# Turning the cross memory's rows: from TensorE to VectorE's 32x32 blocks

## What is computed

```
h = h + merged @ w_out[l]
u = rms_norm(h, norm_xattn_g[l])
mem_n = rms_norm(mem, norm_mem_g[l])               # mem: 256 rows of width 1024
h = h + memory_cross_attention(u, mem_n, ...)

# memory_cross_attention
q = (u @ w_xq) * 128 ** -0.5                       # 4 heads of width 128
kv = mem_n @ w_xkv                                 # keys and values of the 256 rows
s = q k^T per head;  p = softmax(s);  o = p v
return o @ w_xo
```

## Time and profile before

| | |
|---|---|
| median of 3 runs | 1354.56 us (1354.35 to 1354.66) |
| the profiled execution | 1354.18 us |
| its span, first to last instruction | 1352.4 us |
| TensorE busy | 1336.3 us, 99% |
| TensorE weight loads | 1092.6 us, 81% (they overlap the matmuls) |
| VectorE busy | 934.5 us, 69% |
| ScalarE busy | 585.6 us, 43% |
| GpSimd busy | 71.4 us, 5% |
| granted TensorE clock, mean | 1.00 |
| phase w_out | about 295 to 352 us from the span's start |

### The profile page before, as it was taken

The page is one execution under the profiler, slowest core; times in us unless marked ns, Lnnn a source line. Parts: engine busy times, 40 slices in busy tenths (PEclk is TensorE's granted clock), DMA queues, the critical chain, the costliest instruction groups (busy, mean ns, idle before and its releaser), DMA issues.

```text
span 1352.4 us, 17616 instructions
## 1 busy us (share of the span) xinstructions
PE 1336.3 (99%) x6397; PEld 1092.6 (81%) x6397; DVE 934.5 (69%) x1494; ACT 585.6 (43%) x987; POOL 71.4 (5%) x60
## 2 busy tenths in 40 slices
PE   7999999999999999999999999999999999999998
PEld 6787777778888888888888888888888888888886
DVE  7768888785576543355445562598889988995685
ACT  7435655564455432114433344734343433333234
POOL 1000000102002000000013300000000000000000
PEclk9999999999999999999999999999999999999999
DMA  5333233243323333323333333322233223223332
GB/s 163 94 93 79 74 77 84 63 125 109 109 79 94 94 104 113 93 63 111 106 94 93 94 110 93 97 79 84 81 97 94 83 70 95 85 76 109 96 107 94
DMA packets 224104, 127.02 MB, mean 94 GB/s; under 512 B 21234, under 2 KB 214851, under 8 KB 224034
## 3 DMA queue, kind: packets, MB, share of 16 engines
q1 hardware_dynamic: 222418, 123.47, 31.8%
q10 hardware_dynamic: 1616, 2.62, 0.6%
HBM read 123.98 MB, written 2.10 MB: 93 GB/s over the span
## 4 chain that ended last, share of the span: by engine, by line
PE 94%; DVE 3%; ACT 2%; issue 1%; ACTq 0%; DVEq 0%
PE lin L663 26%; PE lin L666 25%; PE lin L667 25%; PE ob L1081 1%; PE sc L746 1%; PE sc L1037 1%; PE sc L1040 1%; PE sc L1041 1%; PE tr L759 1%; PE ob L783 1%; PE sc L770 1%; PE tr L1040 1%; PE lin L1040 1%; PE lin L1041 1%; PE tr L1041 1%
## 5 line engine op out<-in xcount | busy, mean ns | idle before, releaser
L1700 DVE TENSOR_TENSOR wl<-raw,wh 128x1024 fp32r<-128x1024 f32 (+2 forms) x235 | 287.6, 1231 | 64.4 <-ACT wh L1214 59.7
L1214 ACT ACTIVATE wh<-raw 128x1024 fp32r<-128x1024 f32 (+2 forms) x235 | 239.0, 1022 | 132.7 <-DMA raw<-in_w_mlp_dram 44.7
L663 PE MATMUL lin<-uh,wh 128*128 128x512 f32 x624 | 251.2, 402 | 1.3 <-DVE ul L1753 0.9
L667 PE MATMUL lin<-uh,wl 128*128 128x512 f32 x624 | 243.3, 390 | 0.0
L666 PE MATMUL lin<-ul,wh 128*128 128x512 f32 x624 | 243.1, 390 | 0.0
L663 PE MATMUL lin<-vh,wh 128*128 128x512 f32 x512 | 202.6, 396 | 0.2 <-DVE te L2320 0.2
L666 PE MATMUL lin<-vl,wh 128*128 128x512 f32 x512 | 199.6, 390 | 0.0
L667 PE MATMUL lin<-vh,wl 128*128 128x512 f32 x512 | 199.3, 389 | 0.0
L663 PEld LDWEIGHTS lin<-uh,wh 128*128 128x128 f32 x624 | 117.2, 188 | 29.7 <-issue 4.5
L666 PEld LDWEIGHTS lin<-ul,wh 128*128 128x128 f32 x624 | 117.3, 188 | 25.7 <-issue 2.9
L667 PEld LDWEIGHTS lin<-uh,wl 128*128 128x128 f32 x624 | 117.1, 188 | 24.7
(11 more groups left out here) (546 smaller groups left out, 2078.3 us busy)
## 6 DMA issues: line engine op xcount, KB each, us to landing
raw<-in_w_in_dram SPq DMA_DIRECT2D x100, 512.0 KB, 3.8
raw<-in_w_mlp_dram SPq DMA_DIRECT2D x64, 512.0 KB, 3.9
raw<-in_w_out_dram SPq DMA_DIRECT2D x16, 512.0 KB, 3.6
raw<-in_w_xkv_dram SPq DMA_DIRECT2D x8, 512.0 KB, 3.7
raw<-in_w_proj_b_dram SPq DMA_DIRECT2D x8, 512.0 KB, 3.7
raw<-in_w_proj_a_dram SPq DMA_DIRECT2D x8, 512.0 KB, 3.7
xtok<-in_x_dram ACTq DMA_DIRECT2D x4, 512.0 KB, 4.9
raw<-in_w_mla_out_dram SPq DMA_DIRECT2D x4, 512.0 KB, 3.5
```

What stands on the lines that cost most here:

```text
L663: ins = pe.matmul(o, wh[:, slot, at], xh_, start=start, stop=False)
L667: return pe.matmul(o, wl[:, slot, at], xh_, start=False, stop=stop)
L1214: act.activation(wh[:, c.slot(4), 0:size], raw[:, c.slot(2), 0:size], ACT.Copy).then_inc(hi_made, 1)
L1700: dve.tensor_tensor(wl[:, c.slot(4), 0:size], raw[:, c.slot(2), 0:size], wh[:, c.slot(4), 0:size].bitcast(F32), ALU.subtract).then_inc(lo_ ...
```

## The change

`MEM_TURNS`, `turn_memory` and TensorE's calls of it are gone; w_out's jobs run without turns between their matmuls. VectorE turns the memory instead, straight from `memtok` into `memt`, a view of `xp` as 8 feature tiles of 128 x 256. One instruction turns 32 partitions by 512 elements: 16 blocks of 32x32, one for each feature tile and row group. There are 16 of them, five in step m = 0 of w_out, four each in m = 1 and 2, three in m = 3 (`MEM_BLOCKS`), behind the low part of the step's chunk and of the h tile and ahead of the sum to h. VectorE waits for `mem_scaled` at each step. The last one raises `mt_ready`, which now counts to 1.

ScalarE makes all eight `memh` tiles in step m = 3, behind `mt_ready` and ahead of the split of step m = 4. VectorE makes all eight `meml` tiles in step m = 4, behind the chunk's and the h tile's low part and ahead of the sum of job 4. Both read `memt` in on-chip memory where they read a PSUM bank.

```diff
--- before.py
+++ after.py
@@ -109,7 +109,7 @@
 W_ORDER = (("w", 0), ("w", 1), ("w", 2), ("w", 3), ("w", 4), ("k", 0), ("w", 5), ("k", 1), ("w", 6), ("k", 2), ("w", 7),
            ("k", 3))
 
-MEM_TURNS = {0: {2: 0, 4: 1, 6: 2}, 1: {1: 3, 4: 4, 7: 5}, 2: {2: 6, 5: 7}}
+MEM_BLOCKS = {0: (0, 1, 2, 3, 4), 1: (5, 6, 7, 8), 2: (9, 10, 11, 12), 3: (13, 14, 15)}
 CONV_TAPS = (0, 0, 1, 2, 3, 3, 3, 0)
 HEAD_TAPS = (2, 2, 4, 6)
 NCONST = 4 + 16
@@ -283,6 +283,7 @@
         st.close()
         ya = sb("ya", [P, PAIRS, S])
         ybh, ybl = uh, ul
+        memt = xp[:].rearrange("p a q k -> p (a q k)").rearrange("p (f k) -> p f k", f=DT)
         ql, kl = uh[:, PAIRS - 1, :], ul[:, PAIRS - 1, :]
         nlog = sb("nlog", [P, S])
         atok = sb("atok", [P, QT, P])
@@ -913,18 +914,10 @@
                 two_jobs(c + m, j + 2 * m, yh, yl, tiles_of(y_low, 0) if m == 0 else None)
 
 
-            def turn_memory(f):
-
-                pe.wait_ge(mem_scaled, 2)
-                if f >= 3:
-                    pe.wait_ge(mem_low, f - 2)
-                turn_tile(sc[f % 3], lambda q: memtok[:, q, f * P:(f + 1) * P], 2).then_inc(mt_ready, 1)
-
             c, j = phase("w_out")
             for m, (kind, n) in enumerate(W_ORDER):
                 if kind == "w":
-                    job(c + m, j + m, DT, uh, ul, before=tiles_of(m_low, 0) if m == 0 else None,
-                        between={k: lambda f=f: turn_memory(f) for k, f in MEM_TURNS.get(m, {}).items()})
+                    job(c + m, j + m, DT, uh, ul, before=tiles_of(m_low, 0) if m == 0 else None)
                 else:
                     job(c + m, j + m, DT, memh, meml, MEM, tiles_of(mem_low, 0) if n == 0 else None)
 
@@ -1417,10 +1410,11 @@
                     evacuated(act, j + (m - 1))
                     gain_high(xuh[:, f, :], h[:, f, :], col("norm_xattn_g", f))
                     square("xattn", f, h[:, f, :])
-                for f in MEM_TURNS.get(m, {}).values():
-                    act.wait_ge(mt_ready, f + 1)
-                    act.activation(memh[:, f, :], sc[f % 3][:, 0:MEM], ACT.Identity, scale=col("norm_mem_g", f))\
-                        .then_inc(mem_high, 1)
+                if m == 3:
+                    act.wait_ge(mt_ready, 1)
+                    for f in range(DT):
+                        act.activation(memh[:, f, :], memt[:, f, :], ACT.Identity, scale=col("norm_mem_g", f))\
+                            .then_inc(mem_high, 1)
                 if kind == "k":
                     act.activation(xk[:, n, :], read(j + m)[:, 0:MEM], ACT.Copy).then_inc(xk_high, 1)
 
@@ -2011,10 +2005,18 @@
                     f = W_ORDER[m - 1][1]
                     evacuated(dve, j + (m - 1))
                     gain_low(xul[:, f, :], h[:, f, :], col("norm_xattn_g", f), xuh[:, f, :], U0["xattn"] + f + 1)
-                for f in MEM_TURNS.get(m, {}).values():
-                    dve.wait_ge(mem_high, f + 1)
-                    dve.scalar_tensor_tensor(meml[:, f, :], sc[f % 3][:, 0:MEM], col("norm_mem_g", f),
-                                             memh[:, f, :].bitcast(F32), ALU.mult, ALU.subtract).then_inc(mem_low, 1)
+                dve.wait_ge(mem_scaled, 2)
+                for b in MEM_BLOCKS.get(m, ()):
+                    k, i = b // 4, b % 4
+                    ins = dve.transpose(memt[32 * k:32 * k + 32, :, :].rearrange("p f (q i y) -> p q f i y", q=2, i=4)[:, :, :, i, :],
+                                        memtok[32 * i:32 * i + 32, :, :].rearrange("p q (f k x) -> p q f k x", f=DT, k=4)[:, :, :, k, :])
+                    if b == 15:
+                        ins.then_inc(mt_ready, 1)
+                if m == 4:
+                    for f in range(DT):
+                        dve.wait_ge(mem_high, f + 1)
+                        dve.scalar_tensor_tensor(meml[:, f, :], memt[:, f, :], col("norm_mem_g", f),
+                                                 memh[:, f, :].bitcast(F32), ALU.mult, ALU.subtract).then_inc(mem_low, 1)
                 if kind == "w":
                     add_to_h(n, j + m, 0.5)
                 else:
```

## The result

The changed kernel takes **1359.19 us** (median of 8 runs, 1358.52 to 1360.31), the kernel before 1354.78 (8 runs, 1354.35 to 1355.54): ratio 1.0033, 95% interval 1.0024 to 1.0042. It is slower by 4.4 us. The forecast was +2.4 us, 1357.0. The profiled execution took 1359.18 us, its span is 1357.5 us.

A forecast was written before the change was run, and what follows sets the result against it. TensorE, busy 1336.3 of 1352.4 us, was taken as the bound. Removed turns, -1.84 us, plus 4.2 us lost to a stall before job 6 gave +2.4 us, 1357.0 us on the median; range 1352.5 to 1359.9.

The forecast's parts named there:

- Taken from TensorE, 1.84 us: In w_out's first three jobs, eight pairs of turns leave TensorE at 0.23 us each, saving 1.84 us.
- A turn of 32 x 512, 0.72 us: On VectorE in w_out, each of 16 block turns takes 0.72 us, 11.5 us in all.
- the stall: TensorE waits 3.6 us before the first keys job; job 6 then starts late, 4.2 us lost in all.
- Rival A: VectorE's turns are cheap, at most 0.46 us each, so no stall: 1352.7 us; chance 0.12.
- VectorE's chain to mt_ready: VectorE in w_out, m = 0 to 3, runs without waiting from 299.28 and raises mt_ready at 319.5.
- ScalarE's eight at 0.40: At m = 3 ScalarE makes eight high parts in a row, 0.40 us each, 3.2 us, from 319.55 to 322.75.
- the split queued behind them: ScalarE's 1.05 us split for m = 6 follows the high parts, to 323.8; VectorE idles from 320.2 until 323.83.
- VectorE at m = 4: After idling, VectorE makes the chunk's low part, L1753 to 325.63, then eight low parts of 0.40 us, to 328.9.
- rival B: The 3.6 us TensorE wait halves its clock around the keys job, adding 0.8 to 2.3 us; chance 0.12.
- The sum: Whole kernel: -1.84 us of turns plus 4.2 us lost by job 6 gives +2.4 us, 1357.0 us.
- the main forecast: One stall ahead of the keys job, +1.2 to +3.6 us, chance 0.68.
- C: VectorE turns cost 0.80 us or ScalarE's eight 0.48 each: 1358.9 us, 1365.7 at the upper bound; chance 0.06.

The follow-up runs named there:

- The reordered kernel: Changed kernel with ScalarE's split for m = 6 before the eight high parts, and VectorE's h-tile low part after the eight low parts and job 4's sum: 1352.76 us.
- the run with a wait of 3.6 us: Changed kernel with GpSimd's fourth sum of squares in w_out held back until all eight low parts of the memory are made: 1358.75 us, ratio 1.0027.

## Why the prediction was right and wrong

**Taken from TensorE, 1.84 us: right in kind, a little small.** The reordered kernel is 1.9 us faster than the one before, with nothing else of TensorE changed, and the traces show 2.02, 0.25 a pair. The 0.23 was read from the starts at one place, with the matmuls beside the pair counted at 0.23 each.

**A turn of 32 x 512, 0.72 us: right** (0.71 from start to start). The line between two neighbouring forms was the better source than either bound. The Trainium skill's 311 ns, for bf16 ("VectorE: DVE Perf Modes", section "The three transpose paths"), would have made the stall vanish; the trace has a median duration of 0.703 us for as many blocks in float32. Rival A falls with it.

**VectorE's chain to mt_ready, ScalarE's eight at 0.40, and the split queued behind them: right**, each to about 0.1 us. The stop of 3.60 us on VectorE and its cause are there. With the split alone put first, VectorE stopped one instruction later, for the h tile's high part, which is queued behind the same eight; only with both orders mended did the wait go.

**VectorE at m = 4: here a step failed.** "L1753 0.67, to 325.63" took the duration from a place where GpSimd's add always starts 0.3 us after it. In the changed kernel VectorE's step is so late that both come together, and L1747 takes 1.85 us. This is the term that was missing, 1.1 us of TensorE's wait. The forecast looked at GpSimd ("no job of w_out waits for them") only for who waits for its results, not for what it holds while it runs. The Trainium skill has the rule: "SBUF — State Buffer", section "Who interferes with whom", says that a VectorE instruction with two on-chip memory inputs contends with a GpSimd instruction that reads there, and that the order of issue decides which of them blocks the other. The traces agree with the blocking: with the add held back, L1749 is at 0.74, and the instructions that then lie beside the add are long (2.02 instead of 1.22, 1.77 instead of 0.74). Which of the two waits can't be read from the profile's start times: at the same distance of 0.04 us L1747 waits in the changed kernel, and the add waits in the kernel with 18 matmuls. VectorE paid about 1.1 us in each.

**The clock: rival B, given 0.12, is what happened.** It was priced at 0.8 to 2.3 us and cost 0.9 in the changed kernel. The only row behind it was the start's 7.2 us without work, and the prediction gives no other reason for so low a chance. In the run with a wait of 3.6 us the clock fell all the same, and in its profile the keys job and job 6's start were slow for 6.8 us. The Trainium skill, "TensorE: Matmul & The Clock Gate", section "Why this matters for your kernels", warns against such pauses between bursts of matmuls; the profiles of all three kernels here with a pause of 3.3 us or more bear that out, though two of the ten executions of the third have a mean clock of 0.999, as if it had stayed.

**The sum**: forecast -1.84 + 4.2; measured, by the same count, -1.84 + 6.1 (4.71 + 1.40). In the trace job 6 starts 2.0 us later than forecast (332.28 - 0.74 against 329.55): 1.0 because its bank is free later (330.50 against 329.52), which is GpSimd's add, and 1.0 because the keys job is then still running, which is the clock. 1359.19 lies inside the range, near its upper end. That is partly luck: the main forecast stopped at +3.6, rival B had one of the two missing terms, and nothing in the prediction had the other; the range was wide enough for both because B and C had been added to it. "Within 0.2%" had the greatest chance, 0.50, and slower, 0.46, came true; the measured change is clear of 0.2%.

## What to carry to other kernels

Moving work to an engine with room is free only if what is queued behind it, on every engine in the chain, can still come in its old place: with eight short instructions ahead of a weight split on one engine, and the use of their results behind another instruction on the next, the kernel took 6.4 us more than with both put the other way round. The split alone, moved, won 1.2 us; the other order alone was not run. When a step is moved in time, look also at which engine's instruction it will newly lie beside. And price a wait of TensorE with the clock in it: in all three profiles here with a wait of 3.3 us or more ahead of the keys job the granted clock fell, and job 6 began 1.0 to 2.0 us after its bank was free.

## What was not expected of the hardware

- The clock's cost does not follow the length of the wait. In the profiled executions TensorE's wait of 4.7 us had 3.4 us at the lower level (327.6 to 331.0), the wait of 3.6 us had 6.8 (326.0 to 332.8), the wait of 3.3 us 3.4 (328.3 to 331.7), falling only after the matmuls had begun again. With waits of 0.9, 0.8 and 0.6 us it stayed at 1.00. One and the same kernel differs too: with the split first, two of ten executions show a mean clock of 0.999 and took 1.3 us or more less than the other eight. What sets the length, and whether the clock falls at all, was not tried.
- The granted clock is shown as 1.00 at the kernel's start, where the turns are 0.22 us apart and then 0.11; there the granted clock does not show the lower level that the distances do.
- 18 matmuls whose result nobody uses, put into TensorE's wait, made the kernel 0.9 us faster.
- Two instructions that contend and are shown 0.04 us apart, in the same order, can fall out either way: VectorE's waits in one kernel, GpSimd's in the other.
